# The first two of five inversion levels replaced by a column substitution on VectorE, in an RWKV-7 and attention decoder layer

## The reference, cut to what matters

```
def step(S, inp):
    r_t, w_t, k_t, v_t, kk_t, a_t = inp
    sa = jnp.einsum('bhij,bhj->bhi', S, -kk_t)
    S = (S * w_t[:, :, None, :] + sa[..., None] * (kk_t * a_t)[:, :, None, :]
         + v_t[..., None] * k_t[:, :, None, :])
    return S, jnp.einsum('bhij,bhj->bhi', S, r_t)
```

## Time and profile before

| | us |
|---|---|
| median of 3 runs (2980.29 to 2981.38) | 2980.9 |
| the profiled execution's own time | 2979.48 |
| its span, first to last instruction | 2977.4 |
| PE busy in the span | 2905.9 (98%) |
| DVE busy | 916.3 (31%) |
| ACT busy | 950.7 (32%) |
| POOL busy | 1269.2 (43%) |

### The profile page before, as it was taken

How to read it: one execution, slowest core, us unless ns; L and a number is a source line. 1 busy time by engine, 2 the same in 40 slices (tenths; PEclk the granted TensorE clock), 3 DMA queues, 4 the chain that set the end, 5 groups by cost and what they waited for, 6 DMA issues and landing times.

```text
span 2977.4 us, 39855 instructions
## 1 busy us (share of the span) xinstructions
PE 2905.9 (98%) x15752; PEld 2339.6 (79%) x15752; DVE 916.3 (31%) x1404; ACT 950.7 (32%) x1228; POOL 1269.2 (43%) x1020
## 2 busy tenths in 40 slices
PE   8999999999999998999999999999999999999997
PEld 7767777777777776888888888888888888888885
DVE  5666345345255264233321110111101111011123
ACT  5444334333343343222233321333213331122221
POOL 2323323324234234555554444444445444544453
PEclk9999999999999999999999999999999999999998
DMA  5112212212122123433343222322232222322222
GB/s 178 71 71 98 92 62 87 78 61 102 60 79 88 71 79 132 147 141 143 139 156 119 93 86 97 113 99 93 83 106 99 99 94 87 105 94 99 90 92 100
DMA packets 63518, 296.20 MB, mean 99 GB/s; under 512 B 6720, under 2 KB 8000, under 8 KB 39232
## 3 DMA queue, kind: packets, MB, share of 16 engines
q1 hardware_dynamic: 55456, 280.17, 26.7%
q10 hardware_dynamic: 7968, 14.68, 1.3%
HBM read 274.12 MB, written 20.71 MB: 99 GB/s over the span
## 4 chain that ended last, share of the span: by engine, by line
PE 91%; DVE 3%; ACT 2%; issue 2%; POOL 1%; DVEq 0%; DMA 0%; ACTq 0%; SPq 0%; POOLq 0%
PE dense L1217 27%; PE dense L1219 26%; PE dense L1218 26%; PE work L1219 1%; PE work L1218 1%; PE work L1217 1%; PE work L1405 1%; PE work L1425 1%; ACT whi L522 1%; PE work L1378 1%; PE work L1414 1%; DVE Y L1058 1%; PE work L1393 0%; PE work L1470 0%; PE work L1318 0%
## 5 line engine op out<-in xcount | busy, mean ns | idle before, releaser
L484 POOL TENSOR_TENSOR wlo<-raw,whi 128x512 fp32r<-128x512 f32 (+1 forms) x1008 | 1256.6, 1277 | 1675.7 <-ACT whi L522 1675.7
L1217 PE MATMUL dense<-H_hi,whi 128*128 128x512 f32 x2672 | 1077.7, 403 | 18.5 <-DVE H_lo L837 8.9
L1219 PE MATMUL dense<-H_hi,wlo 128*128 128x512 f32 x2672 | 1043.3, 390 | 0.0
L1218 PE MATMUL dense<-H_lo,whi 128*128 128x512 f32 x2672 | 1042.7, 390 | 0.0
L522 ACT ACTIVATE whi<-raw 128x2048 fp32r<-128x2048 f32 (+2 forms) x261 | 456.0, 1748 | 1466.4 <-PE dense L1219 1382.2
L1217 PEld LDWEIGHTS dense<-H_hi,whi 128*128 128x128 f32 x2672 | 502.6, 188 | 147.0 <-issue 35.2
L1219 PEld LDWEIGHTS dense<-H_hi,wlo 128*128 128x128 f32 x2672 | 502.4, 188 | 107.3
L1218 PEld LDWEIGHTS dense<-H_lo,whi 128*128 128x128 f32 x2672 | 503.2, 188 | 100.5 <-issue 5.8
L1219 PE MATMUL dense<-G_hi,wlo 128*128 128x512 f32 x704 | 273.9, 389 | 0.0
L1217 PE MATMUL dense<-G_hi,whi 128*128 128x512 f32 x704 | 273.9, 389 | 0.0
L1218 PE MATMUL dense<-G_lo,whi 128*128 128x512 f32 x704 | 273.9, 389 | 0.0
(11 more groups left out here) (235 smaller groups left out, 2277.7 us busy)
## 6 DMA issues: line engine op xcount, KB each, us to landing
raw<-w_slots SPq DMA_DIRECT2D x101, 1024.0 KB, 4.8
raw<-w_gu SPq DMA_DIRECT2D x88, 1024.0 KB, 4.7
raw<-w_down SPq DMA_DIRECT2D x64, 704.0 KB, 4.0
gates_dram<-gout ACTq DMA_DIRECT2D x32, 256.0 KB, 2.0
gin<-gates_dram SPq DMA_DIRECT2D x16, 512.0 KB, 3.9
X<-xT SPq DMA_DIRECT2D x8, 512.0 KB, 9.9
xin<-xT SPq DMA_DIRECT2D x16, 256.0 KB, 3.5
x_dram<-x ACTq DMA_DIRECT2D x16, 256.0 KB, 3.7
```

The costliest lines, as they stand in the source:

```text
L484: done = nc.gpsimd.tensor_tensor(wlo[s][:, at], raw[s][:, at], whi[s][:, at].bitcast(f32), SUB)
L1217: PE.matmul(bank[:], whi[s][:, wk], hi[:, k, :], start=(k == first), stop=False)
L1218: PE.matmul(bank[:], whi[s][:, wk], lo[:, k, :], start=False, stop=False)
L1219: done = PE.matmul(bank[:], wlo[s][:, wk], hi[:, k, :], start=False, stop=(k == last))
```

## The change

The table `FILL` gets two new places, `gram` (2 steps) and `base` (8 steps), and `rhs` goes from 3 to 2; the two removed levels take 6 steps away, so a pair still does 64. Before the pairs DVE builds three constants: `upper` (the strict upper part within blocks of 8), `block_of` and `place_in`. In a pair:

- the copy of the identity into Y and the eight predicated copies into Y go. ACT now copies L from the bank first, DVE's copy into `lq` waits for it, and PE's reuse of a bank waits for DVE's (`g_read`) in place of ACT's (`l_read`), behind two dense steps;
- DVE masks L to blocks of 8, packs each unit's 128x128 into 8 columns by a reduction over the 16 blocks (`column`), and spreads them over 8x8x8 = 512 columns of `rbuf`;
- one fp32 matmul by `same_block` (128x128 by 128x512) gives each partition the coefficients of all rows of its own block, in R[5]. PE then does 8 dense steps while DVE runs seven substitution steps of a product and a reduction, and one 128x1024 product that unfolds the result into Y;
- the levels run for blocks of 8, 16 and 32 alone (three of five).

```diff
-FILL = {"prep": 4, "tok": 3, "solve": 2, "level_a": 2, "level_b": 1, "join_a": 2, "join_b": 2,
-        "rhs": 3, "u": 3, "state": 2, "y": 2, "center": 2}
+FILL = {"prep": 4, "tok": 3, "gram": 2, "solve": 2, "base": 8, "level_a": 2, "level_b": 1, "join_a": 2, "join_b": 2,
+        "rhs": 2, "u": 3, "state": 2, "y": 2, "center": 2}
...
+    column, partial, inverse = (
+        a_in[:, i * UNITS * BASE:(i + 1) * UNITS * BASE].rearrange("p (w n) -> p w n", w=UNITS)
+        for i in range(3))
+    spread = rbuf[:].rearrange("p (w i k) -> p w i k", w=UNITS, i=BASE)
...
                     for w in range(2 * NB):
-                        act.wait_ge(g_read, p * (2 * NB) + w + 1)
+                        act.wait_ge(g_done, p * (2 * NB) + w + 1)
                         copy(Lt[:, w % 2, w // 2, :], g_bank(w)[:, 0:P]).then_inc(l_read, 1)
+                    fill("gram")
                     fill("solve")
...
+                    fill("base")
+                    for level in range(SOLVE_LEVELS):
...
+            V.tensor_copy(upper[:], masks_f32[:, 0:P])
+            for level in range(BASE_LEVELS):
+                fence()
+                part = second_halves(upper[:], level)
+                V.tensor_tensor(part, part, masks_f32[:, P + level * HALF:P + (level + 1) * HALF]
+                                .rearrange("p (g n) -> p g n", n=2 << level), ADD)
+            fence()
+            V.tensor_tensor(same_block[:], upper[:], ident, ADD)
+            V.tensor_reduce(place_in[:], ident.rearrange("p (b i) -> p i b", i=BASE), AX, ADD)
+            fence()
+            V.tensor_reduce(block_of[:], same_block[:].rearrange("p (b i) -> p b i", i=BASE), AX, ALU.max)
+            fence()
+            V.tensor_copy(same_block[:].rearrange("p (b i) -> p b i", i=BASE),
+                          block_of[:].unsqueeze(2).to_broadcast([P, P // BASE, BASE]))
...
-                    V.tensor_copy(Y[:].rearrange("p e t n -> p (e t) n"), wide(ident, 2 * NB))
...
-                            dve.wait_ge(g_done, p * (2 * NB) + 2 * t + e + 1)
+                            dve.wait_ge(l_read, p * (2 * NB) + 2 * t + e + 1)
                             dve.sem_inc(g_seen, 1)
                             V.copy_predicated(lq[:, e, t].rearrange("p a b -> p (a b)"), lq_keep[:],
-                                              bank[:, P:4 * P])
-                            V.copy_predicated(Y[:, e, t, :], masks[:, 0:P], bank[:, 0:P]
-                                              ).then_inc(g_read, 1)
+                                              bank[:, P:4 * P]).then_inc(g_read, 1)
+                    units = Y[:].rearrange("p e t n -> p (e t) n")
+                    V.tensor_tensor(units, Lt[:].rearrange("p e t n -> p (e t) n"),
+                                    wide(upper[:], UNITS), MUL)
+                    V.tensor_copy(inverse, wide(place_in[:], UNITS))
+                    fence()
+                    V.tensor_reduce(column, units.rearrange("p w (b i) -> p w i b", i=BASE), AX, ADD)
+                    fence()
+                    V.tensor_tensor(column, column, wide(place_in[:], UNITS), ADD)
+                    fence()
+                    V.tensor_tensor(spread, column.unsqueeze(3).to_broadcast([P, UNITS, BASE, BASE]),
+                                    place_in[:].unsqueeze(1).unsqueeze(1).to_broadcast(
+                                        [P, UNITS, BASE, BASE]), MUL).then_inc(spread_ready, 1)
+                    fill("gram")
                     fill("solve")
+                    dve.wait_ge(spread_done, p + 1)
+                    shared = R[5][:].rearrange("p (w i k) -> p w i k", w=UNITS, i=BASE)
+                    for n in range(1, BASE):
+                        V.tensor_tensor(partial[:, :, 0:n + 1], inverse[:, :, 0:n + 1],
+                                        shared[:, :, n, 0:n + 1], MUL)
+                        fence()
+                        V.tensor_reduce(inverse[:, :, n:n + 1], partial[:, :, 0:n + 1], AX, ADD)
+                        fence()
+                    V.tensor_tensor(units.rearrange("p w (b i) -> p w b i", i=BASE),
+                                    inverse.unsqueeze(2).to_broadcast([P, UNITS, P // BASE, BASE]),
+                                    block_of[:].unsqueeze(1).unsqueeze(3).to_broadcast(
+                                        [P, UNITS, P // BASE, BASE]), MUL).then_inc(base_ready, 1)
+                    fill("base")
...
+                        if t == 2:
+                            fill("gram")
                         if t >= 2:
-                            pe.wait_ge(l_read, p * (2 * NB) + 2 * t - 2)
+                            pe.wait_ge(g_read, p * (2 * NB) + 2 * t - 2)
...
+                    pe.wait_ge(spread_ready, p + 1)
+                    PE.matmul(R[5][:], same_block[:], rbuf[:], start=True, stop=True
+                              ).then_inc(spread_done, 1)
+                    fill("base")
                     pe.wait_ge(ln_read, (p + 1) * 2)
-                    for level in range(LEVELS):
+                    pe.wait_ge(base_ready, p + 1)
+                    for at_level, level in enumerate(range(BASE_LEVELS, LEVELS)):
```

More of the change, by code:

```diff
@@ L43 @@
 LEVELS = 5
+BASE = 8
+BASE_LEVELS = 2
+SOLVE_LEVELS = LEVELS - BASE_LEVELS
+assert BASE == 2 << BASE_LEVELS
 HALF = P // 2
@@ L82 @@
             == (FILL_TILE0[_g + 1] - FILL_TILE0[_g]) * KD)
-FILL = {"prep": 4, "tok": 3, "solve": 2, "level_a": 2, "level_b": 1, "join_a": 2, "join_b": 2,
-        "rhs": 3, "u": 3, "state": 2, "y": 2, "center": 2}
-assert (FILL["prep"] + FILL["tok"] + FILL["solve"] + LEVELS * (FILL["level_a"] + FILL["level_b"])
+FILL = {"prep": 4, "tok": 3, "gram": 2, "solve": 2, "base": 8, "level_a": 2, "level_b": 1, "join_a": 2, "join_b": 2,
+        "rhs": 2, "u": 3, "state": 2, "y": 2, "center": 2}
+assert (FILL["prep"] + FILL["tok"] + FILL["gram"] + FILL["solve"] + FILL["base"]
+        + SOLVE_LEVELS * (FILL["level_a"] + FILL["level_b"])
         + FILL["join_a"] + FILL["join_b"] + NB * (FILL["rhs"] + FILL["u"] + FILL["state"])
@@ L204, in build_layer @@
     gout = [rw(f"gout{i}", [T_SEQ]) for i in range(2)]
+    upper, same_block = rw("upper", [P]), rw("same_block", [P])
+    block_of, place_in = rw("block_of", [P // BASE]), rw("place_in", [BASE])
+    column, partial, inverse = (
+        a_in[:, i * UNITS * BASE:(i + 1) * UNITS * BASE].rearrange("p (w n) -> p w n", w=UNITS)
+        for i in range(3))
+    spread = rbuf[:].rearrange("p (w i k) -> p w i k", w=UNITS, i=BASE)
     back = Arena(nc, keep.at)
@@ L278, in build_layer @@
         g_seen, join_seen = sem("g_seen"), sem("join_seen")
+        spread_ready, spread_done, base_ready = (
+            sem("spread_ready"), sem("spread_done"), sem("base_ready"))
         m1_done, rhs_ready, m2_done, u_ready = (
@@ L691, in _ @@
                     copy(lv[:], by_block(R[1][:])).then_inc(lv_read, 1)
-                    for level in range(LEVELS):
-                        act.wait_ge(w1_done, p * LEVELS + level + 1)
+                    fill("base")
+                    for level in range(SOLVE_LEVELS):
+                        act.wait_ge(w1_done, p * SOLVE_LEVELS + level + 1)
                         copy(W1[:], R_half(RW)).then_inc(w1_read, 1)
-                        act.wait_ge(x_done, p * LEVELS + level + 1)
+                        act.wait_ge(x_done, p * SOLVE_LEVELS + level + 1)
                         for e in range(2):
@@ L1045, in _ @@
-                    fill("solve")
-                    for level in range(LEVELS):
-                        dve.wait_ge(x_done, p * LEVELS + level + 1)
+                                              bank[:, P:4 * P]).then_inc(g_read, 1)
[3 more added lines that the diff above has]
+                    V.tensor_copy(inverse, wide(place_in[:], UNITS))
@@ new lines, in _ @@
+                    V.tensor_tensor(units.rearrange("p w (b i) -> p w b i", i=BASE),
[4 more added lines that the diff above has]
+                    for at_level, level in enumerate(range(BASE_LEVELS, LEVELS)):
+                        dve.wait_ge(x_done, p * SOLVE_LEVELS + at_level + 1)
@@ L1053, in _ @@
                         for e in range(2):
-                            dve.wait_ge(p2_done, p * (2 * LEVELS) + 2 * level + e + 1)
+                            dve.wait_ge(p2_done, p * (2 * SOLVE_LEVELS) + 2 * at_level + e + 1)
                             dve.sem_inc(p2_seen, 1)
@@ L1396, in _ @@
                     done.then_inc(lv_done, 1)
+                    pe.wait_ge(spread_ready, p + 1)
+                    PE.matmul(R[5][:], same_block[:], rbuf[:], start=True, stop=True
+                              ).then_inc(spread_done, 1)
+                    fill("base")
                     pe.wait_ge(ln_read, (p + 1) * 2)
-                    for level in range(LEVELS):
-                        if level:
-                            pe.wait_ge(p2_read, p * (2 * LEVELS) + 2 * level)
+                    pe.wait_ge(base_ready, p + 1)
```

(11 more changed lines are left out.)

## The result

The changed kernel takes 2957.64 us in the median of six runs (2954.48 to 2959.16), against 2981.14 (2979.97 to 2982.10) for the kernel before on the same chip: a ratio of 0.9919, 95% interval 0.9907 to 0.9932. The forecast was 2956 in a range of 2941 to 2972. The runs of the changed kernel spread over 4.7 us, those of the kernel before over 2.1: the profile shows why.

What follows compares the result with a forecast made beforehand. PE was taken to bound the kernel (91% of the chain that ended last). Per pair -5.25 - 1.7 + 2.1 + 0.86 + 0.22 + 0.3 = -3.4 us, times 8 -27.3, constants +2.3, total -25.0: 2956 us, range 2941 to 2972.

Steps and rivals of the forecast that it cites:

- The two levels and the switch of the fills: Per pair, two levels removed: -5.25 us; switch into dense steps and back at the new matmul: +0.22.
- The products: Products of tokens (line 1378): line 1389 starts at 7.2 in place of 7.57 with two more dense steps inside, -1.7 us.
- The wait for the spread: PE waits before the new R[5] matmul for DVE's masking, packing and spreading: +2.1 us a pair (0.85 or 4.0 at the ends).
- The substitution: DVE's seven steps and unfolding take 5.2 us after the matmul under 5.7 of base fill: 0, margin 0.5, upper 1.9.
- ACT's tile end: Gate tile 0 ends with the fifth base step; PE waits 0.65 us in place of 0.35 at line 1425: +0.3.
- The constants: Once, ahead of the first pair: seven DVE operations and five drains, +2.3 us, bounds 1 and 4.
- (a): Rival: DVE's packing reduction runs at full rate, 1.25 us less a pair, 2946 us; chance 0.33.
- (b): Rival: DVE's packing pays four elements' time for each, 1.9 us more a pair, 2971 us; chance 0.12.
- (c): Rival: the substitution's short PSUM operations take 0.9 us a step, 1.9 more, margin gone, 2971 us; chance 0.08.
- (d): Slower rival: the substitution, its chain over 5.7 us, runs into POOL's split, up to 4 more than (c), 3003 us; chance 0.05.

Runs made afterwards that it cites:

- e9: Changed kernel with the old order at the products of tokens, no fill between them and the two dense steps put into solve; 2946.24 us, ratio 0.9883.
- e8: Changed kernel with separate DVE reductions, products and predicated copies on scratch data, at various steps and runs, added in two pairs; 2989.61 us in one run.
- e3: Changed kernel with two of the eight base dense steps moved ahead of the new fp32 matmul; 2943.95 us, ratio 0.9882.
- e4: Changed kernel with two dense steps ahead of the new matmul, eight behind; four taken from rhs, two others moved behind turning k, v, b; 2944.67 us.
- e6: Changed kernel with two dense steps ahead of the new matmul, eight behind, four taken from rhs, the two left put in center; 2933.48 us, ratio 0.9843.
- e1: Changed kernel with the packing reduction reading its elements in a row, not every eighth (wrong inverse, time only); 2943.01 us, ratio 0.9874.
- e2: Kernel before, all five levels kept, with only the new order at the products of tokens, its two dense steps taken from rhs; 2991.48 us, ratio 1.0036.
- e10: Changed kernel with the substitution's 14 short operations done three times (wrong inverse, time only); 3024.21 us in one run.
- e7: Changed kernel with the substitution's 14 short operations done twice (wrong inverse, time only); 2999.04 us, ratio 1.0060.
- e5: Kernel before, all five levels kept, with only the new order at the products of tokens, its two dense steps taken from prep; 2974.62 us, ratio 0.9979.

## Why the prediction was right

**The two levels and the switch of the fills.** A level of before, the cost of a switch and the matmul carried over: 736.81 to 743.35 is 6.54 us, and the forecast had 0.86 + 0.22 + 8 x 0.68 = 6.5. A state step went from 6.88 to 6.20 us (762.28 to 768.48 on PE), the one dense step of 0.68 and nothing else.

**The products.** 7.17 for a forecast of 7.2; -1.7 holds. But the forecast priced it against PE's line alone. DVE's chain to the new matmul starts at the end of this stage, and the two dense steps inside it are two that don't cover that chain: with the old order and the steps behind the products, first product to new matmul is 0.66 shorter (e9).

**The wait for the spread.** The term was +2.1, it measured +1.53: the packing takes 2.01 and not 2.5. The term was right in kind and its size came from a row that had nothing to do with it. The slow copy of the first level is slow as a predicated copy, for a product with the same writes isn't (e8), and the rule taken from it (runs of two are dear, single elements perhaps dearer) is not one. The packing is dear for its own reason, a step of 16 bytes or more, and the cost in between the bounds was luck as to the row. The Trainium skill, page "Advanced Engine Details and Errata", section "Memory Cachelines", gives full rate from two hits on a 16-byte line and a penalty where each access has another line. e8 agrees: two fp32 elements to a line take 1.22 us, one to a line 1.97. The forecast held the copy's row against the page; the page was right.

**The substitution.** 0 with a margin of 0.5; measured 0 with 0.36. The short operations take 0.17 to 0.22, as worked out from the rows of 4, 128 and 1024 elements.

**ACT's tile end.** +0.3: the wait is 0.65, as forecast to the last figure, and it is gone in e3, e4 and e6, where the tile ends at another place or PE comes to the level later.

**The constants.** +2.3: they take 2.24 us (239.75 to 241.99 on DVE), and the first products come 2.9 later than before, of which 1.0 was there before the constants.

**What failed is a step that wasn't there.** A pair at full clock takes 112.05 us, 4.0 less than before, where the forecast had 3.4: eight of them give -32.2. The three falls of the clock give back 4.7 and the later start of the products 2.9 (constants and what was late before them), which makes -24.6, where the profiled spans differ by 24.5. The forecast had -25.0 (its terms as printed add to -3.47 a pair, -27.8 in all; it carried on -27.3, a matter of rounding). So the total agrees to a microsecond because an overestimate of the packing (0.5 a pair, 4 us) stood in for the falls (4.7 us), of which the forecast said nothing. It forecast a wait of 2.1 us, where the kernel before has none above 1.1 in the pair it read the earlier trace rows, and did not ask what the granted clock would do behind it. The trace of the kernel before has a case of it, outside the pairs: the clock is at its lower level when PE comes back at 1163.82 from 7.49 us idle.

```profile
1162.00:1165.00 3.00, 1.19 (x3) 1.03 (x4) 2.92 (x2) 3.00 (x7) 3.00 (x4) 0.50 0.48 184
```

e1 is the test: it shortens this wait from 1.53 to 0.74 and moves nothing else, and the falls are gone; e2 has its falls behind another wait, of 1.65 to 2.00. Why three pairs of eight and not the others, with the same 1.53 in each, stays open. The count is not fixed by the wait's length either: at this same matmul, behind 1.52 to 1.54 us in nearly every pair, the traces of e8, e10 and e7 have a fall in 5, 6 and 8 of eight pairs.

**The rivals.** (a) and (b) bracket the packing, and with 2.01 us it fell between (a) and the forecast. (c) is out by the short operations' times. (d), the slower one, is out in both parts: its condition (a chain above 5.7) was not met, and POOL does not hold up operations of these forms (e10). A chain that is too long does end slower than before (e7), by its own length and the clock. The row of 1.18 us in the attention stage is of another form, a tensor-scalar operation; why POOL's time shows there was not tried. A copy shows the same: in the changed kernel DVE's copy of 10 elements ahead of the first pair takes 1.11 us beside POOL (at 241.99, POOL from 241.70 to 247.70), where the kernel before has 0.17 for it with POOL at rest (at 238.87).

## What to carry to other kernels

Where one engine's program is filled by hand with another's work, the place where a tile ends matters as much as the number of steps: the same 64 steps gave 2991 or 2975 us (e2, e5), and 2958, 2945 or 2933 us (the changed kernel, e4, e6), as ACT's tile end stood before an awaited copy or not and as the chain behind a wait was covered. Before placing filler, find the engine that ends last at the next wait and keep filler out of the way of what starts its chain; filler that hides one wait can lengthen a chain that is behind another. And price an idle stretch of TensorE at more than its length: look in the granted clock for what follows it.

## What the runs showed of the hardware that was not expected

- Behind an idle stretch of PE of 1.53 us the granted clock was at the lower level (1.2 GHz) for 3.4 us in three of eight pairs, each about 1.6 us longer (changed kernel); behind one of 1.65 to 2.00 us in three of eight (e2); in e7, with idle stretches of 1.5 to 1.9 and of 2.5 to 3.8 us in a pair, at each of the two in all eight. Behind 0.74 us there was none (e1), nor behind 1.08 to 1.42 us in the profiled run of e3.
- A reduction on VectorE of 1024 fp32 elements takes 1.22 us at a step of 1 and 2 elements, and 1.9 to 2.1 at a step of 4 to 32 elements (e8).
- A predicated copy that writes runs of two takes 0.73 us for 256 elements and a product with the same writes 0.43 (e8).
- With POOL at work, products with one operand in PSUM and reductions of one tensor keep their 0.17 to 0.22 us (e10), while a product of two SBUF tensors went from 1.22 to as much as 2.16 (e7).
